# A decoder-style kernel on one core: the constant mask of the last attention added as two rounded products

## The reference

```
DILATED_BRANCHES = ((128, 1), (512, 4), (2048, 16))
...
    scores = jnp.einsum('brnqhc,brnkhc->brnhqk', qb, kb)
...
    mask = ((dist >= 0) & (dist <= span))[None] & (kpos >= 0)
    scores = jnp.where(mask[None, None, :, None], scores, NEG_INF)
...
def dilated_attention(q, k, v):
    outs = [_dilated_branch(q, k, v, w, d) for (w, d) in DILATED_BRANCHES]
...
    wts = jnp.exp(m_all - jnp.max(m_all, axis=0, keepdims=True))
    num = jnp.einsum('ibsh,ibshc->bshc', wts, acc_all)
    den = jnp.sum(wts * l_all, axis=0)
    return num / den[..., None]
```

## Time and profile before

| | before |
|---|---|
| median of three runs | 3665.62 us |
| the profiled execution, its own time | 3664.48 us |
| its span, first to last instruction | 3662.7 us |
| TensorE busy | 3445.2 us, 94% |
| VectorE busy | 1625.0 us, 44% |
| ScalarE busy | 1172.1 us, 32% |
| GpSimd busy | 611.8 us, 17% |
| mean granted TensorE clock | 0.961 of 2.4 GHz |

### The profile page before, as it was taken

One profiled execution on the slowest core, in us unless ns is written; L12 is line 12 of the kernel. 1 busy time (PEld: TensorE's weight loads), 2 busy tenths in 40 slices (PEclk: granted clock), 3 DMA queues, 4 the chain that ended last, 5 costly groups with the idle time before them and its releaser, 6 DMA issues.

```text
span 3662.7 us, 39900 instructions
## 1 busy us (share of the span) xinstructions
PE 3445.2 (94%) x14476; PEld 2613.6 (71%) x14476; DVE 1625.0 (44%) x2220; ACT 1172.1 (32%) x1728; POOL 611.8 (17%) x388
## 2 busy tenths in 40 slices
PE   7999997999999999998899999899799997879997
PEld 5888763678887888765577888565578875558886
DVE  3332388443323332368644332834433327453323
ACT  4232334433323332334333321213333223443322
POOL 1110234111100110033211100401211004331101
PEclk9999998899999999999799999899899999989999
DMA  4332320023333332331013333340133332223332
GB/s 131 97 92 97 81 75 31 1 70 92 95 94 92 92 96 94 81 80 60 1 41 92 93 96 92 82 84 29 46 92 95 94 92 64 69 60 95 92 97 69
DMA packets 419549, 286.04 MB, mean 78 GB/s; under 512 B 57352, under 2 KB 395116, under 8 KB 419308
## 3 DMA queue, kind: packets, MB, share of 16 engines
q1 hardware_dynamic: 418624, 283.62, 26.7%
q10 hardware_dynamic: 828, 1.13, 0.1%
HBM read 280.24 MB, written 4.47 MB: 78 GB/s over the span
## 4 chain that ended last, share of the span: by engine, by line
PE 87%; DVE 8%; ACT 2%; issue 2%; POOL 1%; DMA 0%; ACTq 0%; DVEq 0%; SPq 0%; POOLq 0%
PE bank L838 24%; PE bank L839 24%; PE bank L840 24%; PE bank L1221 1%; PE bank L1104 1%; PE bank L1105 1%; PE bank L833 1%; PE bank L1123 1%; DVE arena L2017 1%; DVE x L2162 1%; PE bank L1215 1%; DVE arena L1996 1%; DVE small L1993 1%; PE bank L974 0%; PE bank L973 0%
## 5 line engine op out<-in xcount | busy, mean ns | idle before, releaser
L840 PE MATMUL bank<-xn_lo,w_hi 128*128 128x512 f32 x2800 | 1099.9, 393 | 0.0
L838 PE MATMUL bank<-xn_hi,w_hi 128*128 128x512 f32 x2496 | 998.4, 400 | 66.9 <-DVE x L2162 41.7
L839 PE MATMUL bank<-xn_hi,w_lo 128*128 128x512 f32 x2496 | 989.8, 397 | 0.0
L1901 DVE TENSOR_TENSOR w_lo<-wring,w_hi 128x1024 fp32r<-128x1024 f32 x434 | 535.7, 1236 | 908.1 <-ACT w_hi L1467 907.6
L1467 ACT ACTIVATE w_hi<-wring 128x1024 fp32r<-128x1024 f32 x490 | 517.8, 1059 | 1162.8 <-DMA wring<-in_ffn_down 357.6
L840 PEld LDWEIGHTS bank<-xn_lo,w_hi 128*128 128x128 f32 x2800 | 530.2, 189 | 133.0
L838 PEld LDWEIGHTS bank<-xn_hi,w_hi 128*128 128x128 f32 x2496 | 470.2, 188 | 186.9 <-issue 68.6
L839 PEld LDWEIGHTS bank<-xn_hi,w_lo 128*128 128x128 f32 x2496 | 471.2, 189 | 103.9 <-issue 1.4
L839 PE MATMUL bank<-h_hi,w_lo 128*128 (+1 forms) x1056 | 419.6, 397 | 0.0
L840 PE MATMUL bank<-h_lo,w_hi 128*128 (+1 forms) x1056 | 416.5, 394 | 0.0
L838 PE MATMUL bank<-h_hi,w_hi 128*128 (+1 forms) x1056 | 415.4, 393 | 0.0
(11 more groups left out here) (373 smaller groups left out, 3263.1 us busy)
## 6 DMA issues: line engine op xcount, KB each, us to landing
wring<-in_ffn_gate SPq DMA_DIRECT2D x88, 512.0 KB, 3.7
wring<-in_ffn_up SPq DMA_DIRECT2D x88, 512.0 KB, 3.7
wring<-in_ffn_down SPq DMA_DIRECT2D x88, 512.0 KB, 3.5
wring<-in_ffn_w_gate SPq DMA_DIRECT2D x44, 512.0 KB, 3.8
wring<-in_ffn_w_up SPq DMA_DIRECT2D x44, 512.0 KB, 3.7
wring<-in_ffn_w_down SPq DMA_DIRECT2D x44, 512.0 KB, 3.5
wring<-in_w_in SPq DMA_DIRECT2D x34, 512.0 KB, 3.8
wring<-in_w_out SPq DMA_DIRECT2D x16, 512.0 KB, 4.2
```

The costliest lines, as they stand in the source:

```text
L838: nc.tensor.matmul(ps, w_hi[:, slot, t, 0:M], hi, start=start, stop=False)
L839: nc.tensor.matmul(ps, w_lo[:, slot, t, 0:M], hi, start=False, stop=False)
L840: return nc.tensor.matmul(ps, w_hi[:, slot, t, 0:M], lo, start=False, stop=stop)
L1901: nc.vector.tensor_tensor(w_lo[:, slot, :, :].rearrange("p k c -> p (k c)"), wunit[:, slot, :], w_hi[:, slot, :, :].rearrange("p k c -> p ...
```

## The change

The mask and the identity get rounded copies: `one_r` is the identity in `F32R`, `ln_hi` the mask rounded to `F32R`, `ln_lo` the rest. ScalarE makes the first two ahead of the gate's sigmoids, VectorE the third after the rotary sums, in three tiles of the arena that nothing else holds at that time. For the even layer, the one float32 mask product of a unit becomes two `F32R` products, `one_r` with `ln_hi` and `one_r` with `ln_lo`. TensorE's first unit waits for `ln_split` too. The masks of the first block stay one float32 product. The semaphore `fin_ps` of the output's transposes is dropped, and `pro_ps` counts on in its place.

```diff
+        ln_hi, ln_lo = [nc.alloc_sbuf_tensor_at(n, [P, SEQ], F32R, offset=at["arena"] + t * SEQ * 4)
+                        for n, t in (("ln_hi", 22), ("ln_lo", 23))]
+        one_r = nc.alloc_sbuf_tensor_at("one_r", [P, P], F32R, offset=at["arena"] + 24 * SEQ * 4)
...
-        fin_ps = sem("fin_ps")
+        ln_split = sem("ln_split")
...
@@ pe_attention
-                    msk, lo = ops["mask"](m, h, tb, i)
+                    masks, lo = ops["mask"](m, h, tb, i)
...
-                    nc.tensor.matmul(s[:, lo:N], ident, msk, start=False, stop=True).then_inc(att_s.h, 1)
+                    for n, (one, msk) in enumerate(masks):
+                        mm = nc.tensor.matmul(s[:, lo:N], one, msk, start=False, stop=(n == len(masks) - 1))
+                    mm.then_inc(att_s.h, 1)
...
@@ even_ready
             if u == 0:
                 eng.e.wait_ge(glu_sb.h, 4)
+                eng.e.wait_ge(ln_split.h, 1)
...
-        EVEN = dict(qk=even_qk, mask=lambda m, h, tb, u: (C("lnmult")[:, SEQ - (tb + 1) * P:], 0),
+        def even_mask(m, h, tb, u):
+            return [(one_r[:, :], t[:, SEQ - (tb + 1) * P:]) for t in (ln_hi, ln_lo)], 0
+
+        EVEN = dict(qk=even_qk, mask=even_mask,
...
@@ act_even, ahead of the sigmoids
+            nc.scalar.activation(one_r[:, :], ident, ACT.Copy)
+            nc.scalar.activation(ln_hi[:, :], C("lnmult"), ACT.Copy).then_inc(tab_sin.h, 1)
...
@@ the end of dve_even
+            dve.e.wait_ge(tab_sin.h, 5)
+            tt(ln_lo[:, :], C("lnmult"), ln_hi[:, :].bitcast(F32), ALU.subtract).then_inc(ln_split.h, 1)
```

More of the change, by code:

```diff
@@ L1143, in hyb_mask @@
             if m == "D":
-                return C("causal"), tb * P
+                return [(ident, C("causal"))], tb * P
             if tb == 0:
-                return bias[:, h, SEQ - P:SEQ], 0
-            return T(t_bm[BM.index(u) % 3])[:, 0:(tb + 1) * P], 0
+                return [(ident, bias[:, h, SEQ - P:SEQ])], 0
+            return [(ident, T(t_bm[BM.index(u) % 3])[:, 0:(tb + 1) * P])], 0
         def hyb_v(m, h, b):
@@ L1409, in _ @@
                         mm = nc.tensor.transpose(pb[n % 2][:, k * P:(k + 1) * P], x[:, 4 * q + k, tb * P:(tb + 1) * P], ident)
-                    mm.then_inc(fin_ps.h, 1)
+                    mm.then_inc(pro_ps.h, 1)
         LN_EXP = "natural_log_exp_and_others"
@@ L1866, in _ @@
             for n in range(2 * TB):
-                act.e.wait_ge(fin_ps.h, n + 1)
+                act.e.wait_ge(pro_ps.h, 2 + KD + 4 + A_HEADS + n + 1)
                 nc.scalar.activation(arena[:, n, :], pb[n % 2][:, :], ACT.Copy).then_inc(fin_sb.h, 1)
```

## The result

The changed kernel takes 3710.78 us, the median of 20 runs, against 3665.99 us in 20 runs of the kernel before: 1.0107 times as long, interval 1.0085 to 1.0129. The forecast was 3658.6 us, the range 3657.2 to 3662.6. The runs are of two kinds. In 18 of 20 the time lies between 3709.18 and 3712.32 us, in the other two it is 3657.14 and 3659.57 us. The 20 runs of the kernel before all lie between 3664.16 and 3668.38 us.

What follows compares the result with a forecast made beforehand. TensorE, busy 94% of the span, was taken as the bound. Saving 7.1 us over eight heads, less 0.05 for a wait and 0.05 for head 4, gave 7.0: 3665.62 to 3658.6 us, range 3657.2 to 3662.6.

Steps and rivals of the forecast that it cites:

- The price of a mask: Even layer's mask step on TensorE: 0.42, 0.44, 0.55, 0.67 us at the four widths, saving 0.89 us a head.
- Rival (b): Mask products below 512 columns gain nothing, only the widest unit does: 3662.5 us, chance 0.09.
- rival (c): Mask products at 256 and 384 columns cost more than before: up to 3671.1 us, chance 0.04.
- (d): New mask products don't run as rounded ones, each mask streams twice: about 3682 us, chance 0.02.
- rival (a): Rounded mask products stream in half the float32 time, saving 0.965 us a head: 3658.0 us, chance 0.14.
- the floor of 0.11 us a product: Least time of a product with its own weight load, taken for masks at 128 columns: no saving there.
- the 0.1 that was set aside: Head 4, where four weight splits crowd VectorE: at worst 0.1 us lost; 0.05 entered the sum.
- The wait for L1628: TensorE's wait for ScalarE's scaled copy after the widest unit moves forward, keeping its length: 3.2 us in 7 waits.
- The new instructions: ScalarE's copies (0.9 us) and VectorE's subtraction (0.69 us) hide in idle time; TensorE's extra wait costs 0.05 us.
- granted clock 1.00, which is the 2.4 GHz level: The attention stage, 79.70 us with TensorE busy 75.83, read as running at full clock.
- 1.5 us either way: Norm's pause after the output projection: an earlier start may change the low clock's length; taken as 0.
- rival (e): Gain swallowed further on, by VectorE in head 4, other units or the clock after the pause: 3660 to 3664 us, chance 0.05.

Runs made afterwards that it cites:

- a2: Changed kernel with float32 masks in head 0, short (rounded) masks only in heads 1 to 7: 3660.50 us, ratio 0.9988.
- b3: Changed kernel plus three rounded 512-column products in the pause between the gate's last product and the attention: 3658.68 us, ratio 0.998.
- c1: The changed kernel run again, unaltered, in the third set: median 3710.13 us, ratio 1.0078; the clock fell in 9 of 12 runs.
- d1: Kernel before, float32 masks, with one more ScalarE copy ahead of the last sigmoid to lengthen the pause: 3695.37 us, ratio 1.0061.
- b1: Changed kernel with float32 masks in units 0 and 1 of head 0, short ones in the other 30 units: 3659.86 us, ratio 0.9981.
- d2: Changed kernel plus one rounded 512-column product in the pause before the attention: 3659.22 us, ratio 0.998.
- d3: Changed kernel plus one extra rounded product after the masks of unit 0 (256 columns) and unit 1 (512 columns): 3660.24 us, ratio 0.9983.
- c4: Changed kernel plus seven rounded products amid the gate's products, making pause and attention 1.6 us later: 3662.38 us, ratio 0.9989.
- a3: Changed kernel with short masks in head 0 only, float32 masks in heads 1 to 7: 3683.32 us, ratio 1.005.
- a4: Changed kernel plus two rounded 512-column filler products at steps 4, 8, ... 28, in later waits for L1628's copy: 3694.24 us, ratio 1.0077.
- b2: Changed kernel with short masks in units 0 and 1 only, float32 in the other 30: 3666.65 us; the clock fell in 5 of 13 runs.

## Why the prediction was wrong

**The price of a mask was right.** In a2 the clock held, and the chain of waits of a late head reads:

```profile
2549.70 0.63 PE bank L1128 x4
...
2550.96 0.43 PE bank L1109 x2
...
2553.29 0.55 PE bank L1109 x2
...
2555.84 0.68 PE bank L1109 x2
...
2558.39 0.63 PE bank L1128 x4
```

The text had 0.44, 0.55 and 0.67 for the widths 256, 384 and 512, and 0.89 us a head; a head without L1138 takes 8.69 us here (2549.70 to 2558.39) where it took 9.57, 0.88 less. Beside the fixed 0.2 us of a pair, a rounded product's time is thus in proportion to its width from 512 down to 256. Rival (b), narrow products without gain, and rival (c), narrow ones that cost more, are out; so is (d), since one matmul stands per product. Of rival (a) nothing shows: the mask at width 512 is 0.68, not 0.63. At width 128, where the floor of 0.11 us a product had given 0.42, the pair takes 0.37 us against 0.42 for the float32 product; that is hidden, as the text had it. Head 4, crowded by weight splits, takes 8.81 us between VectorE's widest maxima (2529.91 to 2538.72) instead of 8.69, the 0.1 that was set aside. In b3 the stretch from the first score to the projection is 72.5 us against 79.5, the 7.0 of the sum. The wait for L1628 kept its length, in the waits of b3's attention as in the earlier trace rows:

```profile
PE bank L1128 <- ACT arena L1638: 3.4, 7, 1.2
```

The new instructions are hidden as the text had it, in the changed kernel's ScalarE and VectorE in time; the table load ends 6.4 us ahead of the first sigmoid:

```profile
2479.25 0.30 ACT L1745 ACTIVATE one_r<-cst 128x128 fp32r<-128x128 f32 x1
2479.45 0.62 ACT L1746 ACTIVATE ln_hi<-cst 128x512 fp32r<-128x512 f32 x1
2480.08 1.28 ACT L1753 ACT_TABLE_LOAD   x1
2487.76 0.60 ACT L1753 ACTIVATE arena<-bank 128x512 f32<-128x512 f32 x1 [6.39 <-PE bank L1311]
...
2483.67 0.68 DVE L2387 TENSOR_TENSOR ln_lo<-cst,ln_hi 128x512 fp32r<-128x512 f32 x1
```

The five runs of the changed kernel in which the clock held (3657.14, 3659.57, and 3657.3, 3659.37, 3661.43 in c1) have a median of 3659.4 us. The sum was right to within a microsecond for them.

**The step that failed** is the first one: "granted clock 1.00, which is the 2.4 GHz level". It was read as a property of the stage and carried unchanged into the sum; measured, it was 0.50 for 120.3 of the stage's 122.3 us. Only after the stage, in the norm's pause, was the clock given a term, with 1.5 us either way. That the stage itself could lose it stood neither in the sum nor among the rivals, and rival (e) left 0.05 for a gain swallowed further on, not for a loss of 45 us.

**What the runs showed in its place.** The attention's entrance was near the edge already, as d1 shows with the kernel before: a pause 0.5 us longer loses the clock in 8 of 12 runs. The short masks push it over in another way. In unit 0 the two rounded products take 0.37 us where the float32 one took 0.42, but stream, by an estimate from the price of 0.215 us per 128 columns, for 0.11 us instead of 0.215. In unit 1 it is 0.43 us for 0.63, with 0.215 us of streaming instead of 0.43. Beside it stays what doesn't stream, 0.2 us and at width 128 a little more. In the 2 us between the pause and the fall TensorE is in the busy column throughout, and streams less. Give the streaming back anywhere in the entrance, by float32 masks (b1), in the pause (b3, d2) or by rounded filler (d3), and it holds in 11 of 11 runs each, with the moment where it was. Move the same entrance by 1.6 us (c4) and it holds too, so the moment counts as well as the amount. Kernels near the edge fall into two kinds of runs; why one execution falls and the next doesn't stays open.

The Trainium skill says of the monitor behind the clock that it runs freely and doesn't start with the kernel ("TensorE: Matmul & The Clock Gate", Part 1). c4 agrees in so far as the moment doesn't move with the attention. But in six executions of four kernels the fall came within 0.02 us of the same distance from the first score, so here the moment kept its place against the program, and the measurement decides.

Once down, the clock stays down in the attention, whose products don't bring it back reliably: after 41 us in a3, 61 us in d1, 75 us in a4, 129.7 us in b2's profiled run, not at all in the changed kernel. There the dense output projection brings it back in 2.2 us. So a saving of some 0.25 us in the first two units costs 45 us against the kernel before. What exactly brings it back inside the attention stays open. So does the share of units 2 and 3.

**A kernel that beats both.** b3, all masks short and three products in the pause, takes 3658.68 us: 0.998 of the kernel before, interval 0.9971 to 0.9989, in every one of 11 runs. d2, with one product, is as good (3659.22 us, same ratio and interval). Against the kernel before beside them that is 7.7 and 7.2 us: the forecast's gain, a small one of 0.2%, kept by work whose result nobody reads.

## What to carry to other kernels

A stage that runs at the full granted clock has to be checked for how it keeps it before its TensorE work is made shorter: look at its entrance, at the pauses and the narrow products in front, and at what would happen to the whole stage at half clock. Where a stage of many small products follows a pause, filling the pause with products into a free bank is worth a try: here it held the clock in 22 of 22 runs (b3, d2) at no cost that shows. And a time that falls into two kinds of runs calls for the granted clock by stretch before any other view.

## What the runs showed of the hardware that was not expected

- The granted clock fell to half while TensorE was busy, 1.99 us after a pause of only 0.69 us, and in d1 after one of 1.21 us. The Trainium skill ("TensorE: Matmul & The Clock Gate", "Why this matters for your kernels") warns of idle gaps between bursts of matmuls; the only longer gap near by is one of 1.89 us, which ends 16 us ahead of the attention, so its advice doesn't cover this case.
- At half clock TensorE was busy for 20.00 of 20 us in long stretches of the attention and the clock still did not rise, for 120 us in the changed kernel and 129.7 in b2.
- From one execution to the next the clock's changes kept their place against the program: the first fall in the gate came 15.06 to 15.10 us ahead of the first score in twelve traces, from all four sets of experiments.
- Rounded (`F32R`) products of 256 and 384 columns stream in proportion to those of 512: steps of 0.43, 0.55 and 0.68 us for a pair with its fixed 0.2 us. At 128 columns a pair took 0.37 us, the float32 product 0.42.
- Float32 scores and rounded masks are added in one accumulation, and that costs nothing that shows: the fixed part of a mask stays at 0.2 us.
